# Two DeepNorm layers with 64 routed experts: fixed experts packed in three blocks, the slot table made on chip, the first norm tile by tile

## The chip, the core and the metric

The kernel runs on one core of one Trainium2 chip. The metric is the device time of one launch in microseconds (us). The matrix engine is PE (its weight loads PEld), the vector engine DVE, the activation engine ACT, GpSimd POOL, and SP issues most DMAs.

## What is computed

Two layers over 384 tokens (128 of a prompt, 256 of a sample) of width 1024, in float32. Each layer has a mixer (retention, windowed attention, neighbourhood attention) with one projection in and one out, a layer norm, and a mixture of experts with a second norm:

```python
scores = jax.nn.sigmoid(x @ w_router)                       # 384 x 64
emask  = ...                                                # 4 best of 8 groups
_, eidx = lax.top_k(jnp.where(emask, sel, NEG_INF), TOP_K)  # 6 experts a token
wsel = wsel / jnp.sum(wsel, -1, keepdims=True) * ROUTE_SCALE
...
gu  = x[tok] @ w_gu[e]                                      # 1024 -> 512
out = (jax.nn.silu(gu[:, :256]) * gu[:, 256:]) @ w_down[e]  # 256 -> 1024
routed = jnp.zeros_like(x).at[buf_tok].add(out * buf_w)
x = layer_norm(ALPHA * x + g2 * (routed + shared), ln2_g, ln2_b)
```

All 64 experts get tokens (2304 assignments, 36 an expert on average), so the weights of every expert are read in each layer: 2 MB for gate and up, 1 MB for down.

## The kernel before

Everything is written out by hand: five engine programs, one function for each engine in `run_layer`, tied by semaphores; each engine goes through its instructions in program order, and so does SP with its DMAs. The part that the change touches begins at the end of the mixer.

**First norm and routing.** PE multiplies by the output projection, token tile by token tile (L1027, three tiles of 128 tokens, two column halves each). DVE takes each half out of PSUM (L1539), adds the residual (L1508), takes the statistics (L1510 to L1513); ACT takes the root (L1966) and normalizes (L1968). `norm(0, from_psum)` does the statistics of all three tiles first; after it a loop modulates tile 0, 1 and 2 (L1548, L1549) for the experts. PE runs eight filler products (`keep_busy`, L788), then turns each modulated tile (L803), ACT copies it to `xmT` (L1852), and PE makes the router's logits (L1034): those of tile 0 after tiles 0 and 1 are turned, those of tiles 1 and 2 at the end. ACT's sigmoid (L1974) then starts the routing on DVE.

**Plan of the blocks.** Tokens are gathered in blocks of 128 rows. `plan_blocks` fixes beforehand how experts share blocks: experts 0 to 3 have a block of their own each, and the other 60 are ranked by their count of tokens and fill 28 blocks, with one expert (128 rows), two (64 and 64) or three (64, 32 and 32). There are 32 blocks a layer. Within a block the experts' products stand side by side in PE's columns, so that a block costs PE the same with one, two or three experts.

**Slot table.** The slots (which token stands in which row of which block, with what weight) of blocks 0 to 3 are made by one-hots on DVE (L1602) and products on PE (L1071). For the other 28 blocks DVE works out a place for each of the 18 assignments of a partition (L1653 to L1663); POOL writes the entries to a table in HBM with 18 indirect DMAs (L2091), waits for them, reads the table back (L2096), and DVE copies it to `slot_idx`, `slot_tok`, `slot_w` (`take_slots`, L1673 to L1675, after block 2). POOL gathers the rows of each block from `scratch_x` (L2077).

**The loop over blocks.** For block b PE does gate and up (`gate_up`, L1113), adds the rows of block b-2 to their tokens (L1163, L1164), turns the gathered rows of block b+1 (L1100), does down for block b-1 (L1140) and turns the hidden rows of block b (L1125); in between stand pieces of the shared expert (`SHARED_AT`). DVE multiplies the hidden rows (`hidden`, L1729) between gate-up and the turning.

**Weights.** SP loads gate-up weights into a ring of four slots and down weights into six. The load of expert n into its slot (L688) waits until the block of expert n-4 is through gate-up, a down load (L692) until the block of expert n-6 is through down. Experts 0 to 3 are loaded before the ranking is known.

Of the kernel before, what the change touches and what calls it, by code (L numbers as in the profile page):

```python
# [36 lines left out]
PRE = 4  # L37


def plan_blocks():  # L40

    blocks = [[(n, P)] for n in range(PRE)]
    wide, half, third = iter(range(PRE, 12)), iter(range(12, 40)), iter(range(40, E))
    for _ in range(4):
        for kind in (3, 1, 3, 2, 3, 1, 2):
            if kind == 1:
                blocks.append([(next(wide), P)])  # L50
            elif kind == 2:
                blocks.append([(next(half), 64), (next(half), 64)])
            else:
                blocks.append([(next(half), 64), (next(third), 32), (next(third), 32)])
    assert all(next(left, None) is None for left in (wide, half, third))
    return blocks
# [4 lines left out]
LOADS = [r for b in BLOCKS for r, rows in b]  # L61
BLOCK_OF = [n for n, b in enumerate(BLOCKS) for r in b]
# [4 lines left out]
SHARED_AT = {7 + 2 * t + step: (t, step) for t in range(TILES) for step in range(2)}  # L67
SHARED_AT.update({16 + 2 * t + f: (t, 2 + f) for t in range(TILES) for f in range(2)})
SHARED_LOAD, SHARED_DOWN_LOAD, NORM_LOAD = 4, 13, 24
# [25 lines left out]
def constants():  # L95
# [48 lines left out]
    cap, row, col = np.zeros(P), np.zeros(P), np.zeros(P)  # L144
    for n, b in enumerate(BLOCKS):
        for i, (r, rows) in enumerate(b):
            cap[r], row[r], col[r] = rows, sum(other for _, other in b[:i]), n
    put("cap", cap[:, None])
    put("first_row", row[:, None])
    put("column", col[:, None])  # L150
# [46 lines left out]
def build(nc, a, o):  # L197
    soft = [(m, t, h) for t in range(TILES) for m in "BC" for h in (0, 3)]

    with ExitStack() as ctx:  # L200
# [66 lines left out]
        table = c(NB * 2).rearrange("p (b v) -> p b v", v=2)  # L267
# [20 lines left out]
        one_hot = [[c(P) for _ in range(TILES)] for _ in range(PRE)]  # L288
# [6 lines left out]
        wsum = c(8)  # L295
        key_row, rank_at, home, away, room = c(E), c(E), c(E), c(E), c(E)
        key_col = c(2)
        assert c.at <= route_at + 2 * DM + 3 * F

        c = Carve(A, route2_at)  # L300
# [32 lines left out]
        lnb = c(2 * DM).rearrange("p (r d) -> p r d", r=2)  # L333
        shared_gu = B[:, c.at - 4 * DM:c.at].rearrange("p (k n) -> p k n", k=KD)
# [18 lines left out]
        over_part = [ring[3][:, 1536 + CH * (u % 4):2048 + CH * (u % 4)] for u in range(UNITS)]  # L353
        over_idx = nc.alloc_sbuf_tensor_at("over_idx", [P, PASSES * E], I32, offset=begins["ring3"] + 4 * 1024)[:]
# [14 lines left out]
        first_in = c(TILES * PRE * 2).rearrange("p (t e v) -> p t e v", t=TILES, v=2)  # L369
        first_pos = c(TILES * PRE).rearrange("p (t e) -> p t e", t=TILES)  # L370

# [47 lines left out]
        def run_layer(l):  # L419
# [15 lines left out]
            def of_layer(d, name):  # L435
# [27 lines left out]
            table_empty, entries_ready, entries_sent, table_loaded = (  # L463
                sem("table_empty"), sem("entries_ready"), sem("entries_sent"), sem("table_loaded"))
# [12 lines left out]
            first_gathered = [sem(f"first_gathered{b}") for b in range(PRE)]  # L477
# [49 lines left out]
            def gather_of(b):  # L527


                if b < PRE:  # L530
                    return (xg + [gateb[:, 0, :], gateb[:, 1, :]])[b], first_gathered[b], 16
                return xg[b % 2], gathered[b % 2], 16 * ((b - PRE) // 2 + 1)

            def block_loads(b):
                return [n for n in range(E) if BLOCK_OF[n] == b]

# [20 lines left out]
            def _(sp):  # L557
# [157 lines left out]
                for b in range(NB):  # L715
                    if b == 0:
                        sp.wait_ge(entries_ready, 1)
# [11 lines left out]
                    if b == SHARED_LOAD:  # L729
                        sp.wait_ge(residual_ready, TILES)  # L730
# [38 lines left out]
            def _(pe):  # L769
# [374 lines left out]
                def add_rows(b, units):  # L1144


                    for u in units:
                        t, f = u // 2, u % 2
                        bank = psum[UNIT_BANK[u]]
                        if u == 0:  # L1150
                            pe.wait_ge(to_token_ready, b + 1)
                            pe.wait_ge(ys_ready, 2 * (b + 1))
                            if b:
                                pe.wait_ge(added, UNITS * b - 1)
# [1014 lines left out]
```

## Time and profile before

| what | value |
|---|---|
| median of 3 runs (lowest, highest) | 1875.14 us (1873.4, 1878.14) |
| the profiled execution | 1875.72 us, of it 1873.7 us span |
| PE, DVE, ACT busy in the span | 90%, 44%, 21% |
| chain that ended last | PE 35%, DMA 6%, DVE 4% |
| first gate-up of layer 0 and of layer 1 | at 377.7 and 1290.7 us |

The span holds layer 0 up to about 960 us and layer 1 after it. The expert blocks take from 378 to 921 us and from 1291 to 1833 us. The profile's chain lists for each step what released it; its views by windows give the busy time, the clock that PE was granted (PEclk, 1.00 is 2.4 GHz) and the DMA engines' share in a stretch.

### The profile page before, as it was taken

What the parts mean: (1) busy time and instruction counts of PE and PEld (TensorE: products, weight loads), DVE (VectorE), ACT (ScalarE), POOL (GpSimd) and SP (SyncE); (2) the same over time, 40 slices, a digit from 0 to 9 for tenths busy, and PEclk for the clock granted to TensorE, in tenths of its full rate; (3) what the DMA queues carried; (4) which work ended last, traced back from release to release, by engine and by line L of the source; (5) the groups of instructions that cost most, each with busy time, mean ns of one, the idle gap of its engine ahead of it and who ended that gap; (6) DMA issues with size and microseconds to landing.
All of it is one profiled execution on the core that took longest, in us unless ns stands there. A gap on an engine that the chain in (4) does not pass through costs nothing. (4 is left out here: it accounts for less than half of the span.)

```text
span 1873.7 us, 22699 instructions
## 1 busy us (share of the span) xinstructions
PE 1686.7 (90%) x8463; PEld 919.4 (49%) x8463; DVE 819.7 (44%) x1652; ACT 389.6 (21%) x754; POOL 147.5 (8%) x144
## 2 busy tenths in 40 slices
PE   3999999999799799988979999899979989989794
PEld 1885654654344344343448756555434434434342
DVE  2435423654244344342583444255534343444346
ACT  1323531121111111111232324321111111111111
POOL 0000000240000000000010000013200000000001
PEclk8999989799899899999989999997989999999897
DMA  9534527558989999999634443453699899999990
GB/s 354 176 135 147 197 94 267 226 200 357 405 344 400 409 398 417 406 408 422 273 118 129 146 183 107 163 236 120 238 424 405 352 397 391 422 400 398 426 380 34
DMA packets 103470, 538.96 MB, mean 288 GB/s; under 512 B 36830, under 2 KB 39662, under 8 KB 64060
## 3 DMA queue, kind: packets, MB, share of 16 engines
q1 hardware_dynamic: 91996, 515.24, 69.4%
q0 software_dynamic: 11296, 22.14, 3.2%
q8 instruction: 70, 1.15, 0.2%
q14 instruction: 44, 0.36, 0.1%
q10 hardware_dynamic: 64, 0.07, 0.0%
HBM read 545.95 MB, written 6.59 MB: 295 GB/s over the span
## 5 line engine op out<-in xcount | busy, mean ns | idle before, releaser
L1113 PE MATMUL bank<-ring,arena_a 128*32 128x512 f32 (+2 forms) x2432 | 477.1, 632 | 78.4 <-DMA ring<-in_w_expert_gu 77.4
L1113 PEld LDWEIGHTS bank<-ring,arena_a 128*32 128x32 f32 (+2 forms) x2432 | 166.1, 134 | 356.8 <-issue 356.0
L1715 DVE TENSOR_TENSOR arena_a<-arena_a,bank 128x512 f32<-128x512 f32 x336 | 230.5, 686 | 9.7
L1729 DVE SCALAR_TENSOR_TENSOR arena_a<-arena_a,slot_w,bank 128x256 f32<-128x256 f32 x64 | 30.8, 481 | 444.6 <-ACT arena_a L1999 341.1
L1140 PE MATMUL bank<-arena_b,arena_a 128*32 128x512 f32 (+2 forms) x800 | 204.1, 596 | 8.3 <-issue 3.3
L1163 PE MATMUL bank<-ys_hi,to_token 128*128 128x512 f32 x348 | 153.7, 442 | 0.0
L1745 DVE TENSOR_TENSOR ys_lo<-bank,ys_hi 128x512 fp32r<-128x512 f32 x120 | 77.3, 686 | 141.4 <-ACT ys_hi L2007 141.2
L1164 PE MATMUL bank<-ys_lo,to_token 128*128 128x512 f32 x348 | 136.7, 393 | 0.0
L1999 ACT ACTIVATE arena_a<-bank 128x256 f32<-128x256 f32 x64 | 24.6, 384 | 525.8 <-PE bank L1113 525.8
L2077 POOL DMA_INDIRECT arena_a<-scratch_x,slot_idx x60 | 61.0, 1016 | 915.3 <-PE bank L1100 860.0
L881 PE MATMUL bank<-win_hi,xmT_hi 128*128 128x512 f32 (+1 forms) x288 | 109.9, 382 | 14.6 <-DVE arena_a L1335 10.4
L1140 PE MATMUL bank<-arena_a 128*32 128x512 f32 (+2 forms) x416 | 116.4, 595 | 4.4 <-issue 2.2
L2007 ACT ACTIVATE ys_hi<-bank 128x512 fp32r<-128x512 f32 x120 | 65.1, 595 | 218.1 <-PE bank L1140 218.1
L883 PE MATMUL bank<-w_lo,xmT_hi 128*128 128x512 f32 (+1 forms) x288 | 109.6, 381 | 0.0
L882 PE MATMUL bank<-win_hi,xmT_lo 128*128 128x512 f32 (+1 forms) x288 | 109.2, 379 | 0.0
L1140 PEld LDWEIGHTS bank<-arena_b,arena_a 128*32 128x32 f32 (+2 forms) x800 | 64.3, 129 | 76.4 <-issue 74.1
L1027 PE MATMUL bank<-ring,xmT 128*128 128x512 f32 x192 | 86.3, 612 | 6.3 <-ACTq L1961 6.3
L1163 PEld LDWEIGHTS bank<-ys_hi,to_token 128*128 128x128 f32 x348 | 65.4, 188 | 46.2 <-issue 36.3
L1316 DVE TENSOR_TENSOR w_lo<-ring,win_hi 128x2048 fp32r<-128x2048 f32 (+1 forms) x24 | 51.5, 2148 | 80.5 <-ACT win_hi L1867 78.4
L1991 ACT ACTIVATE arena_a<-bank 128x512 f32<-128x512 f32 x64 | 38.3, 598 | 192.2 <-PE bank L1100 192.2
L1164 PEld LDWEIGHTS bank<-ys_lo,to_token 128*128 128x128 f32 x348 | 65.7, 189 | 14.9 <-issue 4.8
L881 PEld LDWEIGHTS bank<-win_hi,xmT_hi 128*128 128x128 f32 x288 | 55.4, 192 | 25.3 <-issue 14.8
(304 smaller groups left out, 2014.7 us busy)
## 6 DMA issues: line engine op xcount, KB each, us to landing
ring<-in_w_expert_gu SPq DMA_DIRECT2D x128, 2048.0 KB, 13.2
arena_b<-in_w_expert_down SPq DMA_DIRECT2D x88, 1024.0 KB, 17.8
ring<-in_w_mod SPq DMA_DIRECT2D x24, 2048.0 KB, 7.8
arena_a<-in_w_expert_down SPq DMA_DIRECT2D x40, 1024.0 KB, 18.1
ring<-in_w_in SPq DMA_DIRECT2D x10, 2048.0 KB, 13.2
ring<-in_w_out SPq DMA_DIRECT2D x4, 2048.0 KB, 8.0
arena_b<-mods SPq DMA_DIRECT2D x8, 512.0 KB, 9.5
arena_a<-mods SPq DMA_DIRECT2D x8, 512.0 KB, 10.0
```

The source lines that it names most:

```text
L881: pe.matmul(out, hi[:, k, :], win_hi[:, k, cols], start=(k == 0), stop=False)
L882: pe.matmul(out, lo[:, k, :], win_hi[:, k, cols], start=False, stop=False)
L883: ins = pe.matmul(out, hi[:, k, :], w_lo[s][:, k, cols], start=False, stop=(k == KD - 1))
L1027: ins = pe.matmul(bank[:, :], xmT[:, k, P * t:P * t + P], w[:, k, :], start=(k == 0), stop=(k == KD - 1))
L1113: ins = pe.matmul(psum[0][r:r + w, :], xT[:, k, r:r + w], ring_view(gu_slot(n))[:, k, :], start=(k == 0), stop=(k == KD - 1))
L1140: ins = pe.matmul(psum[5 + f][r:r + w, :], hT[b % 2][:, k, r:r + w], down[n % ND][:, k, CH * f:CH * f + CH], start=(k == 0), stop=(k == 1))
L1163: pe.matmul(bank[:, :], rows_of, ys_hi[:, cols], start=True, stop=False)
L1164: pe.matmul(bank[:, :], rows_of, ys_lo[:, cols], start=False, stop=True).then_inc(added_full, 1)
L1715: ins = dve.tensor_tensor(z, z, bank[:, :], ALU.add)
L1745: dve.tensor_tensor(lo_of[b][:, cols], psum[5 + f][:, :], hi_of[b][:, cols].bitcast(F32), ALU.subtract).then_inc(ys_ready, 1)
L2007: act.activation(hi_of[b][:, CH * f:CH * f + CH], psum[5 + f][:, :], ACT.Copy).then_inc(ys_high, 1)
L2077: pool.indirect_dma_start(rows_in, None, scratch_x, bass.IndirectOffsetOnAxis(ap=slot_idx[:, b:b + 1], axis=0), bounds_check=TOK - 1, oob_ ...
```

## The change

Four edits, made together. The blocks: experts 0 to 3 get 96 rows each and share three blocks (0 with 1, 1 with 2, 2 with 3), the 60 ranked ones fill 26 blocks, most of them of two or three experts; there are 29 blocks. Expert 1 and expert 2 are used in two blocks, so their ring slots, like that of expert 3, are held up to block 1, 2 and 2. The table: DVE makes for each of the 18 assignments the block (as a row of 29 ones and zeros, with token and weight) and the row (a one-hot of 128), and PE multiplies and sums them in block 1 (`make_table`); POOL's 18 writes and the read go into the branch for overfull experts, which is taken only when an expert has more tokens than rows. Block 2 now needs that table, and is turned after it. The norm: tile 2 is done in halves, tiles 0 and 1 are normalized and modulated while PE multiplies for tile 2, the logits of tiles 0 and 1 come before those of tile 2, and the eight filler products become two. Pieces of the shared expert move two or three blocks ahead.

```diff
+    blocks = [[(0, 96), (1, 32)], [(1, 64), (2, 64)], [(2, 32), (3, 96)]]
+    single, wide, half, third = iter(range(PRE, 5)), iter(range(5, 12)), iter(range(12, 39)), iter(range(39, E))
+    for kind in (2, 4, 3) * 6 + (2, 3, 4, 3, 2, 3, 2, 1):
...
+        elif kind == 4:
+            blocks.append([(next(wide), 96), (next(third), 32)])
...
+LOADS = list(dict.fromkeys(r for b in BLOCKS for r, rows in b))
+BLOCK_OF = [max(i for i, b in enumerate(BLOCKS) if r in [other for other, _ in b]) for r in LOADS]
...
-                keep_busy(("xT", 1, 0, 0), 8)
                 for t in range(2):
-                    pe.wait_ge(xm_ready, t + 1)
                     turn_x(1, t, xm2)
                 pe.wait_ge(wr_loaded, 16)
                 bank = begin(("logit",))
                 logits(bank, 0)
-                pe.wait_ge(xm_ready, TILES)
+                logits(bank, 1)
+                keep_busy(("xT", 1, 2, 0), 2)
                 turn_x(1, 2, xm2)
-                logits(bank, 1)
                 end(logits(bank, 2), ("logit",))
...
+                def make_table():
+                    for t in range(TILES):
+                        pe.wait_ge(rows_hot, t + 1)
+                        for k in range(TOPK):
+                            j = TOPK * t + k
+                            ins = pe.matmul(psum[1][:, 0:2 * NB], in_row[t][:, k, :], placed[:, j].rearrange("p b v -> p (b v)"),
+                                            start=(j == 0), stop=(j == TILES * TOPK - 1))
+                    ins.then_inc(table_full, 1)
...
+                    if b == 1:
+                        make_table()
+                        emptied(5, 6)
+                        down_rows(0)
+                        turn_hidden(1)
+                        turn_rows(2)
+                        continue
...
+                statistics(0, 0, from_psum)
+                statistics(0, 1, from_psum)
+                modulate(0)
+                scale_shift(0, 1)
+                last_half(0)
+                modulate(1)
+                last_half(1)
...
+                scale_shift(0, 2)
+                modulate(2)
...
-                dve.tensor_copy(place_i[:], place).then_inc(entries_ready, 1)
...
+                link(dve.tensor_scalar(block_at, place, 1.0 / P, None, ALU.mult))
+                link(dve.tensor_tensor(past, over_blocks(block_at, NB + 1), columns(NB + 1), ALU.is_ge))
+                link(dve.tensor_reduce(column_at, past[:, :, 1:NB + 1], AX.X, ALU.add))
...
+                link(dve.tensor_tensor(in_block, past[:, :, 0:NB], past[:, :, 1:NB + 1], ALU.subtract))
...
+                    dve.tensor_tensor(in_row[t], const("slot").unsqueeze(1).to_broadcast([P, TOPK, P]),
+                                      row_at[:, TOPK * t:TOPK * t + TOPK].unsqueeze(2).to_broadcast([P, TOPK, P]), ALU.is_equal).then_inc(rows_hot, 1)
...
-                    dve.wait_ge(table_loaded, 16)
...
+                    dve.wait_ge(table_full, 1)
...
-                for j in range(TILES * TOPK):
-                    pool.indirect_dma_start(slots, bass.IndirectOffsetOnAxis(ap=place_i[:, j:j + 1], axis=0),
...
-                pool.dma_start(table, by_row[:, 0:NB, :]).then_inc(table_loaded, 16)
```

PE's program around block 1, before: block 2's rows were turned and its gate-up stood right behind down of block 0 and the turning of block 1's hidden rows (`ring` is the gate-up weights, `arena_b` the down weights).

```order
L1140 MATMUL bank<-arena_b,arena_a 128x512 [waits hT_ready,down_ready0,bank_free6,bank_free5]
L1140 MATMUL bank<-arena_b,arena_a 128x512 x3
L1125 MATMUL bank<-cst,arena_a 128x128 [waits hT_ready,hid_ready]
L1125 MATMUL bank<-cst,arena_a 128x128
L1113 MATMUL bank<-ring,arena_a 128x512 [waits ring_ready2,hid_ready,xT_ready]
```

The same place now: after gate-up of block 1 the 18 products of the table (L1127), down of block 0, and only then the turning of block 2's rows (L1118), which waits for their gather.

```order
L1141 MATMUL bank<-ring,arena_a 64x512 [waits ring_ready1,ring_ready2,hid_ready,xT_ready]
L1141 MATMUL bank<-ring,arena_a 64x512 x15
L1127 MATMUL bank<-arena_a,arena_b 128x58 [waits rows_hot]
L1127 MATMUL bank<-arena_a,arena_b 128x58 x5
L1127 MATMUL bank<-arena_a,arena_b 128x58 [waits rows_hot]
L1127 MATMUL bank<-arena_a,arena_b 128x58 x5
L1127 MATMUL bank<-arena_a,rows 128x58 [waits rows_hot]
L1127 MATMUL bank<-arena_a,rows 128x58 x5
L1168 MATMUL bank<-arena_b,arena_a 32x512 [waits down_ready0,hT_ready,down_ready1,bank_free6,bank_free5]
L1168 MATMUL bank<-arena_b,arena_a 32x512 x15
L1153 MATMUL bank<-cst,arena_a 128x128 [waits hT_ready,hid_ready]
L1118 MATMUL bank<-cst,arena_a 128x128 [waits xT_ready,gathered0]
```

So gate-up of block 2 now stands behind a gather that itself stands behind the table.

DVE's program at the end of the first norm, now, from the last column half of tile 2 (L1595) on: half the width is left to add and to take statistics of, and one modulation (L1583, L1586) instead of the three that stood here before.

```order
L1595 TENSOR_TENSOR arena_a<-bank,arena_b 128x512 [waits bank_full5,xm_ready]
L1597 SCALAR_TENSOR_TENSOR arena_a<-x,arena_a 128x512 [waits dve_step]
L1598 BN_STATS cmisc<-arena_a 128x6 [waits dve_step]
L1607 BN_AGGR cmisc<-cmisc 128x2 [waits dve_step]
L1608 TENSOR_SCALAR cmisc<-cmisc 128x1 [waits dve_step]
L1553 RECIPROCAL cmisc<-cmisc 128x1 [waits lroot_ready]
L1554 TENSOR_SCALAR cmisc<-cmisc 128x1 [waits dve_step]
L1583 TENSOR_TENSOR arena_a<-arena_a 128x1024 [waits normal_ready]
L1586 TENSOR_TENSOR arena_a<-arena_a 128x128x4 [waits dve_step]
L1586 TENSOR_TENSOR arena_a<-arena_a 128x128x4
```

The modulations of tiles 0 and 1 have moved ahead of the last column half, where DVE waited for PE.

## Rows read from the trace of the kernel before

**Rows 1.** The page: span, and its costliest group with the waits before it.

```profile
span 1873.7 us, 22699 instructions
...
L1113 PE MATMUL bank<-ring,arena_a 128*32 128x512 f32 (+2 forms) x2432 | 477.1, 632 | 78.4 <-DMA ring<-in_w_expert_gu 77.4
```

**Rows 2.** Windows, expert stages: length, PE/PEld/DVE/ACT/POOL busy (count), PEclk, DMA share, GB/s.

```profile
440.00:460.00 20.00, 19.74 (x103) 9.36 (x105) 9.42 (x20) 3.64 (x7) 0.99 (x1) 1.00 1.00 423
382.00:440.00 58.00, 57.10 (x245) 29.64 (x244) 29.23 (x54) 10.85 (x23) 23.44 (x23) 1.00 0.66 240
560.00:914.00 354.00, 323.19 (x1734) 149.14 (x1726) 141.64 (x270) 50.54 (x100) 17.79 (x18) 0.96 0.99 408
382.00:914.00 532.00, 488.97 (x2511) 228.81 (x2509) 215.04 (x409) 78.57 (x157) 47.16 (x47) 0.96 0.94 385
1296.00:1826.00 530.00, 484.52 (x2495) 225.17 (x2493) 214.83 (x406) 78.43 (x155) 47.90 (x47) 0.96 0.94 384
```

**Rows 3.** Timeline of PE, layer 0, blocks 2 and 3: start, us, engine, line.

```profile
398.40 7.03 PE L1113 MATMUL bank<-ring,arena_a 128*128 128x512 f32 x16
...
407.12 1.03 PE L1100 MATMUL bank<-cst,arena_b 128*128 128x128 f32 x8
...
409.47 3.67 PE L1140 MATMUL bank<-arena_b,arena_a 128*128 128x512 f32 x8 [0.39 <-DVE arena_a L1713]
413.19 7.03 PE L1113 MATMUL bank<-ring,arena_a 128*128 128x512 f32 x16
```

**Rows 4.** Timeline of the first norm's end in layer 1: DVE, PE, ACT.

```profile
1240.01 0.69 DVE L1539 TENSOR_TENSOR arena_a<-bank,arena_b 128x512 f32<-128x512 f32 x1 [5.61 <-PE bank L1027]
1242.11 1.29 DVE L1510 BATCH_NORM_STATS2 cmisc<-arena_a 128x6 f32<-128x512 f32 x2
...
1244.42 1.22 DVE L1548 TENSOR_TENSOR arena_a<-arena_a 128x1024 f32<-128x1024 f32 x1
1244.54 1.24 ACT L1968 ACTIVATE arena_a<-arena_a,cmisc 128x1024 f32<-128x1024 f32 x1 [0.48 <-DVE cmisc L1519]
1245.67 1.92 DVE L1549 TENSOR_TENSOR arena_a<-arena_a 128x1024 f32<-128x1024 f32 x1
...
1255.10 1.92 PE L803 MATMUL bank<-cst,arena_a 128*128 128x128 f32 x8
1256.80 4.54 PE L1034 MATMUL bank<-arena_a,xmT 128*128 128x64 f32 x32
1261.38 0.33 ACT L1974 ACTIVATE arena_a<-bank 128x192 f32<-128x192 f32 x1 [2.35 <-PE bank L1034]
```

**Rows 5.** Windows of layer 1 from the logits through the routing.

```profile
1250.00:1262.00 12.00, 11.15 (x66) 10.77 (x67) 4.28 (x6) 4.00 (x6) 4.71 (x6) 0.72 0.36 143
1272.00:1282.00 10.00, 10.00 (x44) 8.63 (x43) 4.53 (x22) 0.00 (x0) 0.00 (x0) 0.50 0.00 0
```

**Rows 6.** Timeline of layer 0: POOL's first table write and first table gather, DVE's first hidden rows.

```profile
382.48 1.02 POOL L2091 DMA_INDIRECT slots<-arena_a,place_i  x1 [7.85 <-DVE place_i L1663]
...
385.31 0.48 DVE L1729 SCALAR_TENSOR_TENSOR arena_a<-arena_a,slot_w,bank 128x256 f32<-128x256 f32 x1 [2.83 <-ACT arena_a L1999]
...
416.48 1.05 POOL L2077 DMA_INDIRECT arena_a<-scratch_x,slot_idx  x1 [6.11 <-DVE slot_w L1675]
```

**Rows 7.** DMA issues of the page: count, KB each, median us to landing.

```profile
ring<-in_w_expert_gu SPq DMA_DIRECT2D x128, 2048.0 KB, 13.2
...
arena_a<-scratch_x,slot_idx POOLq DMA_INDIRECT x60, 10.6
...
arena_b<-scratch_x,slot_idx POOLq DMA_INDIRECT x4, 3.5
```

**Rows 8.** The chain that ended last, layer 1, around a wait for weights: start, us, what.

```profile
1717.77 7.11 PE bank L1113 x64
1728.17 25.29 DMA ring<-in_w_expert_gu
1753.60 8.74 PE bank L1113 x64
```

More of the change, by code:

```diff
@@ L37 @@
 PRE = 4
+PREB = 2
+FIXED_ROOM = 96
+FIRST_PARTS = [(0, 0), (1, 0), (1, 1), (2, 1)]
+OVER = 4096
 def plan_blocks():
[L45 to L55, printed above, removed]
+    blocks = [[(0, 96), (1, 32)], [(1, 64), (2, 64)], [(2, 32), (3, 96)]]
+    single, wide, half, third = iter(range(PRE, 5)), iter(range(5, 12)), iter(range(12, 39)), iter(range(39, E))
+    for kind in (2, 4, 3) * 6 + (2, 3, 4, 3, 2, 3, 2, 1):
+        if kind == 1:
+            blocks.append([(next(single), P)])
+        elif kind == 4:
+            blocks.append([(next(wide), 96), (next(third), 32)])
+        elif kind == 2:
+            blocks.append([(next(half), 64), (next(half), 64)])
+        else:
+            blocks.append([(next(half), 64), (next(third), 32), (next(third), 32)])
+    assert all(next(left, None) is None for left in (single, wide, half, third))
     return blocks
@@ L266, in build @@
         hT = [c(F).rearrange("p (k t) -> p k t", k=2) for _ in range(2)]
-        table = c(NB * 2).rearrange("p (b v) -> p b v", v=2)
+        block_at, column_at, row_at = (c(TILES * TOPK) for _ in range(3))
         place, most_f = c(TILES * TOPK), c(8)
@@ L1086, in _ @@
                 pe.wait_ge(ranks_ready, 1)
-                for i, name in enumerate(("cap", "first_row", "column")):
+                for i, name in enumerate(("cap", "home")):
                     pe.matmul(bank[:, E * i:E * i + E], const(name)[0:E, :].to_broadcast([E, P]), rank_is[0:E, :], start=True, stop=True)
-                end(pe.matmul(bank[:, 3 * E:4 * E], const("up")[0:E, :].to_broadcast([E, P]), rank_at[0:E, :], start=True, stop=True), ("where",))
+                end(pe.matmul(bank[:, 2 * E:3 * E], const("up")[0:E, :].to_broadcast([E, P]), rank_at[0:E, :], start=True, stop=True), ("where",))
                 assert next(turn, None) is None
@@ L1542, in from_psum, with modulate @@
                             scale_shift(which, t - 1)
-                norm(0, from_psum)
-                for t in range(TILES):
+                def modulate(t):
                     c_ = 0 if t == 0 else 1
@@ L1845, in late_rows, with turned @@
                     act.dma_start(mods[:, n // 2, CH * (n % 2):CH * (n % 2) + CH], stage[n % 2]).then_inc(stage_sent[n % 2], 16)
[L1847 to L1848 removed]
+                def turned(*tiles):
+                    for t in tiles:
                         for g in range(2):
@@ L1961, in _, with norm @@
                     act.sem_inc(yT_ready, 1)
-                def norm(which):
-                    for t in range(TILES):
+                def norm(which, *tiles):
+                    for t in tiles:
                         act.wait_ge(lvar_ready, TILES * which + t + 1)
```

212 lines of the change are left out of this document (136 added, 76 removed).

## The prediction

> **What bounds the kernel now.** I read the page first, then windows, then the timeline at the three places that the change touches. The page shows PE as the busy engine and gate-up as its costliest line, with 78 us of idle time before it that ended with a weight load [rows 1]. So PE isn't the only limit. The windows say where the other one is [rows 2]: over layer 0's expert stage (382 to 914 us, from the first load of a ranked expert to the landing of the last) the DMA engines are 0.94 busy at 385 GB/s, and from 560 on 0.99 busy at 408 GB/s. Layer 1's stage looks the same (530 us, 0.94, 384 GB/s). The reader is to see that late in the stage nothing more fits into the queues, while the opening (382 to 440) has a share of 0.66 and 240 GB/s: there PE was nearly always busy (57.1 of 58 us) and the queues waited for ring slots.
>
> In this opening a block takes 14.8 us: gate-up starts at 398.40 and again at 413.19, with 7.03 us of gate-up, 3.67 of down and 1.03 for turning rows, the rest being additions [rows 3]. Three blocks fewer are therefore 3 x 14.8 = 44.4 us of PE a layer. How much of that is time depends on the weights, whose bytes don't change.
>
> As bytes: 532 us x 385 GB/s = 204.8 MB; at 408 GB/s these need 502 us, so 30 us of layer 0's stage are lost to an idle queue. The opening moved 58 x 240 = 13.9 MB, worth 34 us, so 24 of the 30 are lost there; the other 6 come later.
>
> Measurement tells a change of 0.3% (5.6 us) from none. My sums are made against the profiled execution (1875.72 us, 1873.7 of it the span [rows 1]); the median of the runs is 0.6 us below it.
>
> **The norm.** Before, DVE gets PE's last column half at 1240.01 and the sigmoid starts at 1261.38: 21.4 us [rows 4], in which PE waits. After the change what is left behind that half is: gating 0.69, residual on half the width 0.69 (the gating has that size), one of two statistics 0.65, the small steps up to ACT 1.1 (1243.40 to 1244.54), normalizing 1.24, multiplying 1.22, the addition in two halves 1.92, the second half's turning 0.96 (half of 1.92), ACT's copy 0.6 (half a normalization), one tile's logits 2.27 (half of 4.54), and six hand-overs between engines, for which I allow 0.15 each (0.04 lie between the last logits and the sigmoid), 0.9 [rows 4]. That is 12.2 us, a gain of 9.2. Tiles 0 and 1 are modulated where DVE sat idle for 5.61 us [rows 4] and earlier. Against it: ACT copies four half tiles (2.5 us) ahead of the last root, and PE's two fillers stand ahead of tile 2. Low end 6 us, high end 10.5 (PE at the full clock); I take **9**, near the sum. The sums of the keys, ranks and counts that follow change by less than 1 us beside PE's work and are costed at nothing; if PE ran faster there, DVE's longer list of first slots (four small instructions for one) would show, 0.6 us.
>
> The eight fillers that go are the other side. PE was granted 0.72 of its clock over 1250 to 1262 and 0.50 over 1272 to 1282 even with them [rows 5], so the lengths above are already those of a PE that is partly at 1.2 GHz, and taking the fillers away can cost the matrix part (0.96 + 2.27) once more at most; the low end holds that.
>
> **The table.** POOL's 18 writes, the wait and the read (from 382.48 until the first gather from the table at 416.48 [rows 6]) go. They weren't on PE's path, since block 4 was the first to need them, but block 2 now is. DVE's new list: five instructions of 522 or 540 elements at 0.7 (512 take 0.69), three of 768 at 0.95 (between 0.69 for 512 and 1.22 for 1024) [rows 4] and a few small ones, 6.9 us, less some 2 for ten small ones that go: 4 to 7, I take 5. DVE was idle for 2.83 us before the first hidden rows at 385.31 [rows 6], so these come at 387.5, 2.2 late, and so does gate-up of block 1 (388.7 to 395.8, in the clock of layer 0 before). The table is 18 products of two passes each; 36 x 0.142 (4.54 / 32 [rows 4]) = 5.1 us, up to double at the lower clock: 400.9. Down of block 0 and turning take 4.1: PE is free at 405. The gather is issued at 401.5 and lands 3.5 us (few other loads) to 10.6 us (the queues full) later [rows 7], at 405 to 412; I take 408, since only one weight load is under way. Turning 1.03 [rows 3], ACT's copy 1.2 and hand-overs: gate-up of block 2 runs from 410.5 to 417.6. Before, block 2 ran at 398.40 and block 3 until 420.2 [rows 3]: with a block fewer the change is 2.6 us ahead there.
>
> **The weight stream.** Up to the end of block 2 only two ring slots come free (after blocks 0 and 1), because the slots of experts 2 and 3 are held. From 382 to 419.6 (417.6 and an estimated 2 us until packets flow, below the 3.5 us in which the quickest gathers land [rows 7]) the queues get two gate-up and two down loads, 6.3 MB (2048 KB a gate-up load [rows 7], half of that a down load), and some 0.6 MB of gathers: 17 us of work at 408 GB/s, so 20.6 are lost, less 2 because the places are ready that much earlier. After that the stream should not stop: three blocks take seven experts, 22 MB and 1 MB of gathers, 56 us, against 3 x 14.8 = 44.4 of PE; I allow 2 us. Lost: 18.6 + 2 = 21 instead of 30, **9 a layer**, and 1 off for a tail in which the last block stands further behind its weights: **8**. So 44.4 us of PE work buy 8, and the rest becomes waiting for weights at gate-up: that is late next. The shared expert's pieces, 2 or 3 blocks earlier, cost nothing under these waits; without them they'd be the same work at another place.
>
> Low end of this part: 0, with a gather of 10.6 us, a table at twice its price; high end 26: all 204.8 MB at the 423 GB/s of 440 to 460 [rows 2], 484 us.
>
> By the Trainium skill (DMA: Bandwidth & Descriptors, Specifications) a core gets about 358 GB/s of HBM; the stage would need 204.8 / 0.358 = 572 us whatever the blocks, and only the norm's gain would be left. The trace doesn't agree: 408 GB/s were held for 354 us [rows 2], and the sum goes by that.
>
> **Sum.** 2 x (9 + 8) = 34; 1875.7 - 34 = 1841.7, and 1841 for the median.
>
> **Rivals.**
> - *The stream runs full.* If a queue that never empties runs at 423 GB/s throughout [rows 2], 18 us a layer more: 1841 - 36 = 1805. For it: every idle gap lowers the 408 too. Against: at a share of 0.99 there is little to gain. Chance 0.20.
> - *The weights swallow the blocks.* A late gather of block 2 and a table at the lower clock (0.50 in the stretch before it [rows 5]) lose in the opening what the three blocks give; only the norm's 9 a layer stay: 1875 - 18 = 1857. For it: PE waits for weights already [rows 1], and block 2's chain has no cover. Against: it takes both at their high ends. Chance 0.20.
> - *Slower: waits lower the clock, and the ring feels it.* With 56 us of weights to 44.4 of PE some 20 blocks a layer wait. After a wait of 25.29 us gate-up took 8.74 us, not 7.11 [rows 8], and its slots come free 1.6 us later. If the queue is empty by then, each such wait lengthens the stage: 20 x 1.63 = 33 us a layer, 1841 + 66 = 1907; from 13 such waits a layer (2 x (17 - 13 x 1.63) + 0.3%) it is slower than before. For it: the rows. Against: two or three down loads (2.6 us each) stand in the queue behind the gate-up loads and keep it fed over 1.6 us, and the 408 already holds such waits. Chance 0.05. By the Trainium skill (TensorE: Matmul & The Clock Gate, HAM oscillation) a matmul loop that waits for loads falls back to the lower clock each time; the trace agrees (8.74 against 7.11 [rows 8]).
> - *The change doesn't do what it says.* More tokens than rows would start the branch for overfull experts, 192 passes long. The reference's own routing gives at most 68 tokens to a fixed expert (96 rows), 107 to the first ranked one (128), 55 to rank 12 (64 rows), 29 to rank 39 (32 rows). Chance 0.01.
>
> **Chances and range.** The forecast, 1826 to 1856, has 0.51; the two faster rivals 0.20 each; both gains lost to small things, within 0.3%, 0.03; slower 0.05 + 0.01. Faster is 0.51 + 0.20 + 0.20 = 0.91, same 0.03, slower 0.06. The range reaches to 1808 (most of the first rival lies above or near it) and to 1864 (the second rival and a norm at its low end, 1875 - 12 = 1863); about 2 in 10 stay outside.
>
> **What would show it.** Right: sigmoid to last column half some 12 us, not 21; 29 groups of gate-up a layer; DMA share near 1 from block 3 to the end, 0.4 to 0.5 before; idle time before gate-up that ends with weights well over 78 us; gate-up of block 2 some 33 us behind that of block 0. Wrong: a stage shorter than 500 us (first rival), of 530 or more (second), or DMA gaps right after long waits at gate-up (third); or POOL's table writes in the trace.

## The result, and the profile after

The changed kernel takes 1830.25 us (median of 4 runs, 1826.82 to 1832.7) where the kernel before takes 1876.64 (1873.4 to 1882.23): a ratio of 0.9748, 95% interval 0.9718 to 0.9779, faster. The prediction was 1841 with 1826 to 1856 for the forecast. A second set of runs, on another occasion, gave 1831.85 and 0.9757 (0.9732 to 0.9783).

The profiled execution has 46.9 us less span than before [rows 1]. The page of the changed kernel, its span, chain and costliest group:

```profile
span 1826.8 us, 23899 instructions
...
PE 32%; DMA 9%; DVE 5%; ACT 1%; issue 1%; SPq 0%; ACTq 0%; DVEq 0%; POOLq 0%
...
L1141 PE MATMUL bank<-ring,arena_a 128*32 128x512 f32 (+2 forms) x2976 | 446.7, 644 | 114.1 <-DMA ring<-in_w_expert_gu 111.3
```

Gate-up is busy for 446.7 us, not 477.1 [rows 1], and waits 111.3 us for weights, not 77.4: in both layers together gate-up is 30 us shorter, and 34 us of new waiting for weights came. Where the 46.9 us went, by marks in the two timelines:

| stretch | before, us | after, us | gained |
|---|---|---|---|
| start to the first output product, layer 0 | 285.7 | 280.9 | 4.8 |
| PE's end of the last column half to sigmoid, layer 0 and 1 | 21.4, 21.4 | 12.1, 12.0 | 18.7 |
| sigmoid to first gate-up, layer 0 and 1 | 27.4, 29.3 | 27.6, 27.5 | 1.6 |
| first to last gate-up, layer 0 and 1 | 543.5, 542.4 | 532.4, 532.3 | 21.2 |
| all else | 402.5 | 402.0 | 0.5 |

The expert stage, windows of the changed kernel (length, busy time of PE, PEld, DVE, ACT and POOL with counts, PEclk, DMA share, GB/s); they answer to [rows 2]:

```profile
367.00:425.00 58.00, 54.16 (x364) 24.94 (x360) 29.22 (x53) 8.83 (x20) 4.95 (x5) 0.97 0.71 274
425.00:540.00 115.00, 108.95 (x658) 47.54 (x651) 43.98 (x85) 16.67 (x34) 5.95 (x6) 0.99 0.99 407
540.00:888.00 348.00, 295.77 (x1863) 127.66 (x1865) 126.21 (x240) 45.33 (x89) 15.86 (x16) 0.93 0.99 408
367.00:888.00 521.00, 458.89 (x2880) 200.14 (x2876) 199.41 (x378) 70.82 (x141) 26.76 (x27) 0.94 0.96 393
1258.00:1779.00 521.00, 458.25 (x2864) 198.34 (x2856) 199.53 (x379) 70.57 (x139) 27.23 (x27) 0.95 0.95 391
```

521 us at 393 GB/s are the same 204.8 MB. The queue is full from 425 on at the same 408 GB/s as before; only the opening has a hole (0.71), and PE is now 85% busy late in the stage, where it was 91%. In the kernel before, the queue lost some us after its opening too, in this stretch:

```profile
440.00:560.00 120.00, 108.67 (x539) 50.03 (x541) 44.17 (x87) 17.18 (x34) 5.93 (x6) 0.96 0.93 386
```

The opening of layer 0, timeline of PE, DVE and POOL:

```profile
363.60 7.07 PE L1141 MATMUL bank<-ring,arena_a 128*32 128x512 f32 x64 [0.30 <-issue]
...
374.38 7.09 PE L1141 MATMUL bank<-ring,arena_a 128*64 128x512 f32 x32
381.40 2.89 PE L1127 MATMUL bank<-arena_a,arena_b 128*128 128x58 f32 x24
384.12 1.50 PE L1127 MATMUL bank<-arena_a,rows 128*128 128x58 f32 x12
385.56 3.64 PE L1168 MATMUL bank<-arena_b,arena_a 128*32 128x512 f32 x32
...
390.76 1.10 PE L1118 MATMUL bank<-cst,arena_a 128*128 128x128 f32 x8 [1.19 <-DMA arena_a<-scratch_x,slot_idx]
393.03 8.77 PE L1141 MATMUL bank<-ring,arena_a 128*32 128x512 f32 x64 [1.17 <-ACT arena_a L2098]
...
373.42 0.47 DVE L1832 SCALAR_TENSOR_TENSOR arena_a<-arena_a,slot_w,bank 128x256 f32<-128x256 f32 x1
...
386.80 0.99 POOL L2185 DMA_INDIRECT arena_a<-scratch_x,slot_idx  x1 [28.22 <-DVE slot_w L1753]
```

The chain is the one foretold: table, gather, turning, gate-up of block 2. PE waits twice in it, 1.19 and 1.17 us, and gate-up then takes 8.77 us instead of 7.09 (over 393.6 to 403.6 us PE was granted 0.85 of its clock).

The end of the first norm in layer 1, timeline of DVE, PE and ACT, from the last column half to the sigmoid; it answers to [rows 4]:

```profile
1214.71 0.69 DVE L1595 TENSOR_TENSOR arena_a<-bank,arena_b 128x512 f32<-128x512 f32 x1 [0.99 <-PE bank L1046]
1215.55 0.69 DVE L1597 SCALAR_TENSOR_TENSOR arena_a<-x,arena_a 128x512 f32<-128x512 f32 x1
...
1219.89 1.23 DVE L1583 TENSOR_TENSOR arena_a<-arena_a 128x1024 f32<-128x1024 f32 x1 [1.31 <-ACT arena_a L2072]
1221.15 1.95 DVE L1586 TENSOR_TENSOR arena_a<-arena_a 128x512 f32<-128x512 f32 x2
...
1224.60 2.00 PE L1053 MATMUL bank<-arena_a,xmT 128*128 128x64 f32 x16 [0.73 <-ACTq L1959]
...
1226.63 0.33 ACT L2080 ACTIVATE arena_a<-bank 128x192 f32<-128x192 f32 x1 [0.75 <-PE bank L1053]
```

11.9 us from 1214.71 to 1226.63 (12.0 from PE's end, as in the table). The chain of waits late in layer 1 (1600 us to the end; first its shares by line, then one piece of it: start, us, what):

```profile
by line: DMA ring<-in_w_expert_gu 49.6%; PE bank L1141 42.7%; PE bank L1168 2.0%; SPq L728 1.9%; issue 1.6%; PE bank L1193 0.9%; PE bank L1194 0.8%; PE bank L1118 0.5%; SPq L704 0.3%; PE bank L1153 0.2%
...
1675.79 8.05 DMA ring<-in_w_expert_gu
1683.84 0.14 issue
1683.97 7.11 PE bank L1141 x64
1691.10 0.27 SPq L728
1691.39 0.15 SPq L728
1691.82 13.29 DMA ring<-in_w_expert_gu
1705.24 9.77 PE bank L1141 x64
```

This is a loop: gate-up lets a ring slot go, SP issues the load into it, gate-up of a later block waits for that load. Both halves of the loop are in the chain, although the queue is full all the while. So a longer gate-up here is not free, and a faster PE elsewhere is not worth its whole time. A load's length in this chain runs from its issue to its landing; PE's own wait, in its timeline, is shorter:

```profile
1683.97 7.07 PE L1141 MATMUL bank<-ring,arena_a 128*32 128x512 f32 x64 [0.91 <-DMA ring<-in_w_expert_gu]
...
1705.24 9.73 PE L1141 MATMUL bank<-ring,arena_a 128*32 128x512 f32 x64 [6.27 <-DMA ring<-in_w_expert_gu]
```

The granted clock was 1.00 in the first of these gate-ups and 0.72 in the second.

### The profile page after: what moved, and what is told of

It is laid out like the page before. It is cut to its first block and busy times, and to the rows that moved or that the text cites. A ratio compares the mean times of both kernels' runs of the same rounds, so it can differ in the third digit from the quotient of the medians.

```text
span 1826.8 us, 23899 instructions
## 1 busy us (share of the span) xinstructions
PE 1607.3 (88%) x9191; PEld 848.1 (46%) x9191; DVE 790.5 (43%) x1598; ACT 374.5 (20%) x724; POOL 98.6 (5%) x96
## 5 line engine op out<-in xcount | busy, mean ns | idle before, releaser
L1141 PE MATMUL bank<-ring,arena_a 128*32 128x512 f32 (+2 forms) x2976 | 446.7, 644 | 114.1 <-DMA ring<-in_w_expert_gu 111.3
L1141 PEld LDWEIGHTS bank<-ring,arena_a 128*32 128x32 f32 (+2 forms) x2976 | 138.0, 124 | 394.8 <-issue 392.0
L1818 DVE TENSOR_TENSOR arena_a<-arena_a,bank 128x512 f32<-128x512 f32 x300 | 205.7, 686 | 8.7
L1168 PE MATMUL bank<-arena_b,arena_a 128*32 128x512 f32 (+2 forms) x1040 | 189.3, 595 | 5.1 <-DVE arena_a L1841 2.1
L1193 PE MATMUL bank<-ys_hi,to_token 128*128 128x512 f32 x312 | 132.8, 426 | 0.0
L1848 DVE TENSOR_TENSOR ys_lo<-bank,ys_hi 128x512 fp32r<-128x512 f32 x108 | 69.5, 686 | 125.5 <-ACT ys_hi L2113 125.4
L1194 PE MATMUL bank<-ys_lo,to_token 128*128 128x512 f32 x312 | 123.1, 394 | 0.0
L1168 PE MATMUL bank<-arena_a 128*32 128x512 f32 (+1 forms) x448 | 101.7, 595 | 1.5 <-issue 0.2
L1168 PEld LDWEIGHTS bank<-arena_b,arena_a 128*32 128x32 f32 (+2 forms) x1040 | 56.4, 116 | 84.2 <-issue 81.6
L1118 PE MATMUL bank<-cst,arena_a 128*128 128x128 f32 x464 | 62.0, 278 | 3.1 <-DMA arena_a<-scratch_x,slot_idx 3.1
## 6 DMA issues: line engine op xcount, KB each, us to landing
arena_b<-in_w_expert_down SPq DMA_DIRECT2D x88, 1024.0 KB, 18.5
arena_a<-mods SPq DMA_DIRECT2D x8, 512.0 KB, 10.3
```

What stands on the lines that cost most here:

```text
L1118: ins = pe.transpose(psum[2 + k // 4][:, P * (k % 4):P * (k % 4) + P], rows_in[:, P * k:P * k + P], ident)
L1141: ins = pe.matmul(psum[0][r:r + w, :], xT[:, k, r:r + w], ring_view(gu_slot(n))[:, k, :], start=(k == 0), stop=(k == KD - 1))
L1168: ins = pe.matmul(psum[5 + f][r:r + w, :], hT[b % 2][:, k, r:r + w], down[n % ND][:, k, CH * f:CH * f + CH], start=(k == 0), stop=(k == 1))
L1193: pe.matmul(bank[:, :], rows_of, ys_hi[:, cols], start=True, stop=False)
L1194: pe.matmul(bank[:, :], rows_of, ys_lo[:, cols], start=False, stop=True).then_inc(added_full, 1)
L1818: ins = dve.tensor_tensor(z, z, bank[:, :], ALU.add)
```

## The experiments

Times are medians; "of before" is the ratio to the kernel before on the same chip, with its 95% interval.

**The changed kernel once more, for comparison.** 

> The changed kernel as it is, for comparison on the same chip: 1830 us, 1826 to 1833. If the 4.8 us that the changed kernel's mixer of layer 0 was quicker belong to the change, the first output product of layer 0 starts 5 us sooner than in the kernel before here too; if they are chance of the clock, it can stand anywhere within those 5 us.

1831.85 us, 0.9757 (0.9732 to 0.9783). In its profiled execution the first output product of layer 0 stood at 286.7 us, where the first profile had 280.9 and the kernel before 285.7. The other eleven profiles of this study, whose mixers are the same, fall into the same two groups, whatever the kernel: 280.5 to 281.7 in seven of them, 285.6 to 286.3 in four. So the 4.8 us in the table above aren't the change's. Windows of the two first profiles (before, then after) show what differs, PE's clock (0.76 and 0.88):

```profile
250.00:285.00 35.00, 30.21 (x175) 17.35 (x173) 3.57 (x12) 13.65 (x32) 0.00 (x0) 0.76 0.16 61
```

```profile
250.00:281.00 31.00, 24.52 (x171) 14.13 (x163) 3.16 (x9) 13.45 (x32) 0.00 (x0) 0.88 0.18 69
```

The expert stage differs between the two profiles of the changed kernel as well. The second was taken of an execution of 1842.21 us, and its stages are 538.3 and 532.5 us long, where the first has 532.4 and 532.3: gate-up of block 1 alone took 8.49 us in layer 0 and not 7.09, at a granted clock of 0.83. So what the stage of layer 0 gained is between 5 and 11 us, that of layer 1 is 10 us in both, and a difference of a few us between single profiles in the runs that follow isn't shown to be of the edit.

**The norm undone in the changed kernel.** DVE's and ACT's order, the whole-tile modulation, the logits and eight fillers as before:

```diff
+                keep_busy(("xT", 1, 0, 0), 8)
...
-                logits(bank, 1)
-                keep_busy(("xT", 1, 2, 0), 2)
                 turn_x(1, 2, xm2)
+                logits(bank, 1)
...
-                statistics(0, 0, from_psum)
-                statistics(0, 1, from_psum)
...
+                norm(0, from_psum)
+                for t in range(TILES):
+                    modulate(t)
```

> The changed kernel with the first norm, its modulation, the eight fillers and the order of the logits as in the kernel before; blocks and table stay as changed. Theory (PE waits for the norm, and nothing behind it makes up for a later start): last column half to sigmoid 21.4 us again, 9.4 a layer more, 1849 (1845 to 1852). Rival (the expert stage, bound by weights whose first loads wait already, gives part of it back): under 1840.

1859.22 us, 0.9902 (0.9873 to 0.9931): 0.0145 x 1876 = 27 us more than the changed kernel, not 19. From the last column half to the sigmoid it is 21.6 us in both layers, 19 us more together, as expected, and the expert stage gives nothing back (534.8 and 534.1 us against 532.4 and 532.3). In the profiled execution (1869.19 us, 10 above this run's median) another 12 us lie between the experts of layer 0 and the output products of layer 1, in code that wasn't touched, where PE was granted 0.78 and 0.74 in two stretches and the changed kernel 0.97 and 0.91.

**The norm alone in the kernel before.** The same edit the other way. 

> The kernel before with the new norm alone (order of the norm, half tiles, logits, two fillers); 32 blocks and the table through memory. Theory (the norm is worth its own stretch, 9.4 us a layer, in either kernel): 1857 to 1858. Rival (the 27 us that its undoing cost in the changed kernel are all its own): 1849.

1851.5 us, 0.9882 (0.9860 to 0.9904): 22 us less than the kernel before. Its norm takes 12.3 and 12.0 us, 18.5 of the 24.3 us by which its profiled span is shorter; 4.0 are the mixer of layer 0 again (281.7), and 3.2 the stretch from sigmoid to gate-up. Its expert stages are those of the kernel before (543.8 and 543.3 us). So the norm's gain takes nothing from the experts' and is 18.5 to 19 us by its own stretch in both kernels; whether the 3 to 8 us beyond it belong to the norm (a PE that waits less, and keeps its clock) or to chance isn't settled by these two runs.

**The old plan with the new table and norm.** 

> The changed kernel with the plan of the kernel before: 32 blocks, one fixed expert each, the shared expert's pieces at their old blocks; norm and table stay as changed. Theory (the weights set the pace; three blocks fewer are worth what the opening's queue loses without them): with one ring slot a block, 402 to 432 us of layer 0 moves some 5 MB instead of 12, so 17 us a layer are lost there: 1864 (1852 to 1876). Rival (PE sets the pace, and the blocks' 44.4 us a layer are time): 1918.

```diff
-FIXED_ROOM = 96
-FIRST_PARTS = [(0, 0), (1, 0), (1, 1), (2, 1)]
+FIXED_ROOM = 128
+FIRST_PARTS = [(0, 0), (1, 1)]
...
-    blocks = [[(0, 96), (1, 32)], [(1, 64), (2, 64)], [(2, 32), (3, 96)]]
+    blocks = [[(n, P)] for n in range(PRE)]
```

1869.97 us, 0.9954 (0.9936 to 0.9972): 38 us above the changed kernel, so three blocks fewer, with the shared expert's pieces moved along with them (this run puts those back too), are worth 19 us a layer, not 44. The run also prices the table, since its plan is that of before. PE in the opening:

```profile
361.36 7.11 PE L1140 MATMUL bank<-ring,arena_a 128*128 128x512 f32 x16 [0.36 <-issue]
...
389.96 1.09 PE L1117 MATMUL bank<-cst,arena_a 128*128 128x128 f32 x8 [0.89 <-DMA arena_a<-scratch_x,slot_idx]
392.23 7.13 PE L1140 MATMUL bank<-ring,arena_a 128*128 128x512 f32 x16 [1.18 <-ACT arena_a L2097]
```

Gate-up of block 2 starts 30.9 us behind that of block 0, where the kernel before has 20.7 (398.40 [rows 3] less 377.7). The stage is 554.6 and 552.3 us long, 10 to 11 more than before, and that difference is there by block 7 (115.1 against 104.9 us) and stays to the end. With 32 blocks, then, the table on the chip is a loss of 10 us a layer in this profile. The times say somewhat less: this run is the kernel before with the new norm and the new table, the last one the kernel before with the new norm alone, and 0.9954 less 0.9882 is 13.5 us, 7 a layer. The fewer blocks pay for it and bring 10 to 12 us on top.

**The table twice.** `for t in list(range(TILES)) * 2` in `make_table`. 

> The 18 products of the table are made twice, the second time into the same bank from the start. That is 4.2 us more of PE between gate-up of block 1 and the gather for block 2. Theory (block 2 has no cover, and the next two weight loads wait for its end): gate-up of block 2 ends 4.2 us later, the two loads behind it start 4.2 us later, and the end of the stage moves by the same: 8.4 us in all, 1838 to 1839. Rival (the waits for weights later in the stage swallow what the opening loses): no change, 1830.

1838.77 us, 0.9805 (0.9776 to 0.9834), some 7 to 9 us above the changed kernel, as the theory said, but the intervals touch and the profile doesn't show it where it should be: gate-up of block 2 ended 1.2 us later in layer 0 and 3.4 in layer 1, not 4.2, since it started 2.9 and 4.9 us later and took 7.1 us in both, not 8.8 and 8.6 (why it was quicker isn't shown); the two stages (530.3 and 535.0 us) are together 0.6 us longer than those in the first profile of the changed kernel; 10 us lie between the layers (285.6 us for 275.6), where nothing was edited. What the table's products cost, between nothing and their 4.2 us a layer, isn't settled.

**Fillers in each block.** 

> The changed kernel with eight filler products (128x512) ahead of each gate-up from block 3 on, after its wait for rows and before its wait for weights: 26 x 8 x 0.214 = 44.5 us of PE a layer more, about what three blocks cost. Theory (from block 3 on the weights set the pace, and PE's idle time before gate-up, 55 us a layer, takes the fillers): at most 6 us a layer more, 1830 to 1842. Rival (PE sets the pace): 89 us more, 1919.

```diff
+                    if b > 2:
+                        for _ in range(8):
+                            pe.matmul(psum[0][:, :], ident, cst[:, 0:CH], start=True, stop=True)
                     for n in loads:
                         pe.wait_ge(ring_ready[gu_slot(n)], 16 * gu_loads(n))
```

2046.26 us, 1.0898 (1.0865 to 1.0931), 214 more than the changed kernel. The expectation had the price of a filler wrong, as the page of this run shows (832 records, two to a product, 365.6 us: 0.88 us a product, not 0.214):

```profile
L1144 PE MATMUL bank<-ring,arena_a 128*32 128x512 f32 (+2 forms) x2976 | 418.2, 603 | 2.4 <-ACT arena_a L2101 2.3
L1139 PE MATMUL bank<-cst 128*128 128x512 f32 x832 | 365.6, 592 | 0.0
```

So 366 us of work were put in and 214 came out. Most of the other 152 are what the changed kernel had left on PE: the 111 us of waits for weights (all gone, 2.4 of any kind are left) and 28 us of gate-up at a lower clock (446.7 to 418.2). Here PE is the limit, and the stream isn't:

```profile
425.00:888.00 463.00, 461.25 (x2413) 199.55 (x2415) 141.88 (x272) 51.91 (x102) 19.77 (x20) 1.00 0.83 336
```

**Two fillers instead of eight.** 

> As the run with eight fillers, but with two: a product of 128x512 in this kernel is 7.07 / 8 = 0.88 us (gate-up is eight of them), not the 0.214 that the first expectation took, so 26 x 2 x 0.88 = 46 us of PE a layer, what three blocks cost. Theory (PE's idle time before gate-up, 55 us a layer, takes them): at most 7 us a layer more, 1830 to 1845. Rival (PE sets the pace): 92 us more, 1922.

1856.83 us, 0.9912 (0.9891 to 0.9934): 25 more by the medians and 29 by the ratios, 12 to 15 a layer, for 49 us of fillers a layer (97.8 us in the page's group). A quarter to 30% comes through, more than the 7 us that were allowed: half of the waits for weights (52.5 us) are still there, but the fillers stand in the loop of ring slots also where weights had landed. Neither engine alone sets the pace at this point.

**Half the bytes.** The load of each expert beyond those in the first ring and down slots is cut to its first half, in the changed kernel and in the one before. 

> The changed kernel with half the bytes: from the fifth expert on only half of a gate-up load and from the seventh on half of a down load is made, so the products use old weights in the other half (that part of the computation is left out). Theory (with weights out of the way PE sets the pace): idle time before gate-up that ends with weights falls from 111 us to under 15, and the time to 1715 to 1740.

> The kernel before with the same half loads (the same part of the computation left out). Theory (the three blocks are real PE time that the weights hide): 80 to 108 us slower than the changed kernel with half loads, instead of the 46 that it is with full loads: 1800 to 1840. Rival (the blocks save no more PE time than was seen): 46 us slower than that kernel.

1691.28 us (0.9017, 0.8943 to 0.9090) and 1780.41 us (0.9492, 0.9419 to 0.9564). The pages, first the changed kernel, then the one before:

```profile
L1143 PE MATMUL bank<-ring,arena_a 128*32 128x512 f32 (+2 forms) x2976 | 413.8, 598 | 4.6 <-ACT arena_a L2100 2.3
```

```profile
L1115 PE MATMUL bank<-ring,arena_a 128*32 128x512 f32 (+2 forms) x2432 | 452.2, 594 | 0.9 <-ACT arena_a L1994 0.6
```

With no waits for weights the two kernels are 89 us apart, not 46, and their stages 457.5 and 461.4 against 491.3 and 491.2 us: 32 us a layer, about three blocks of 14.8 less the table's chain. So the change takes that much off PE, and the waits for weights (71 to 75 us a layer above this floor in the changed kernel, 51 or 52 in the one before) hide two thirds of it. Both times are some 20 us below what was expected, their difference is not.

**Earlier loads in the opening.** The queue's hole in the changed kernel lies at 0.62 and 0.16 from 383.6 to 403.6 us, because SP stands at the wait for block 2. 

> Only SP's order is changed: the shared expert's gate-up weights (2 MB) and the first down load whose slot comes free (1 MB) are issued before SP waits for the end of gate-up of block 2, not behind the two loads that wait for it. Theory (what the opening leaves the queue idle is lost for the stage): 3 MB at 408 GB/s, 7.4 us a layer, move into the idle part at 389 to 402 us, and each layer's stage is 5 to 7.5 us shorter: 1815 to 1820. Rival (the stage's length is set later, by PE or by waits in the middle): 1830, no change. Rival (the early loads disturb the gather for block 2 or 3): slower than 1830.

1825.29 us, 0.9729 (0.9704 to 0.9754): about 5 us less, a third to a half of the expectation, and the intervals overlap, so the time alone doesn't show it. Windows of 10 us, before and after the point where the changed kernel's hole ended:

```profile
387.90:397.90 10.00, 8.40 (x73) 5.23 (x71) 3.58 (x11) 1.29 (x3) 1.98 (x2) 1.00 0.82 281
397.90:407.90 10.00, 9.07 (x67) 2.61 (x68) 3.98 (x4) 1.27 (x3) 1.98 (x1) 0.83 0.85 300
407.90:417.90 10.00, 9.84 (x49) 4.89 (x49) 6.83 (x13) 2.17 (x4) 0.99 (x1) 1.00 1.00 401
417.90:427.90 10.00, 9.94 (x58) 4.95 (x58) 4.76 (x9) 1.47 (x3) 0.99 (x1) 1.00 0.63 229
```

The early 3 MB did move, and then the queue was dry again for 3.7 us, since block 3 had not yet let its slots go. Block 6 started 3.9 us sooner than in the changed kernel (100.3 against 104.2 after block 0; 4.1 sooner in layer 1), which is what 7.4 us won and 3.7 given back would leave.

**Three moves in the opening.** The table ahead of gate-up of block 1, the residuals and loads earlier still:

```diff
+                    if b == 1:
+                        make_table()
                     gate_up(b)
...
                         residual(0)
+                        take_slots()
                         residual(1)
...
+                    if b in (1, 2):
+                        sp.wait_ge(y_full, BLOCK_OF[b - 1] + 1)
+                        load_down(ND + b - 1, loaded(ND + b - 1))
```

> Three moves in the opening of the changed kernel: PE makes the table ahead of gate-up of block 1 (in the 1.3 us in which it waits, and 3 more) and turns block 2's rows ahead of down of block 0; DVE adds the last two residuals before the hidden rows of block 1, so that SP can issue the shared expert's 2 MB at about 384 us, ahead of the second ranked gate-up load; two down loads are issued as soon as their slots are free. Theory (the run with early loads gained 3.9 us a layer by block 6 and not 7.4, because its queue ran dry again at 421 to 424, before gate-up of block 3 let the next loads go): with the loads 10 us earlier and gate-up of block 2 ending 3 to 4 us sooner the queue should not run dry after 384: 7 to 10 us a layer off the changed kernel, 1810 to 1817. Rival (each hole only moves to the next place): 1823 to 1827, as with early loads alone.

1820.94 us, 0.9720 (0.9698 to 0.9742): 9 to 11 us below the changed kernel by the medians, 5 to 7 by the ratios, and the best of all versions, though its interval still overlaps that of the changed kernel. Block 6 starts at 97.4 us, 6.8 sooner (94.5 in layer 1, 10.3 sooner). The profiled execution took 1814.05 us, the least of the five. The ranked experts' weights take 515.5 and 507.7 us from the first issue to the last landing, against 519.3 and 519.5 (525.5 and 519.3 in the second profile of the changed kernel).

**Two more down loads earlier.** 

> The run with three moves in the opening left one hole: from 429.5 to 434 us of layer 0 the queue moved 12 and 81 GB/s, because SP waits for gate-up of block 4 while two more down slots have been free since 424. Here these two down loads (2 MB, 4.9 us at 408 GB/s) go ahead of that wait. Theory (a hole in the opening is lost for the stage): 4 to 5 us a layer off that run, 1811 to 1814 by its median of 1820.9. Rival (from here on PE or the waits in the middle set the pace): no change, 1821.

1829.46 us, 0.9752 (0.9724 to 0.9780): by the medians the gain is lost again, though this interval and that of the run with three moves overlap. Windows of the run with three moves, then of this one:

```profile
429.00:434.00 5.00, 5.00 (x40) 2.90 (x30) 2.29 (x4) 0.38 (x1) 0.00 (x0) 1.00 0.37 102
...
452.00:456.00 4.00, 4.00 (x30) 1.61 (x23) 1.62 (x5) 1.09 (x2) 0.00 (x0) 1.00 1.02 434
```

```profile
429.00:434.00 5.00, 5.00 (x52) 1.43 (x44) 0.30 (x1) 0.00 (x0) 0.00 (x0) 1.00 1.00 418
...
440.00:452.00 12.00, 9.43 (x64) 3.25 (x64) 1.86 (x5) 1.08 (x2) 0.00 (x0) 0.86 0.97 408
452.00:456.00 4.00, 4.00 (x28) 2.31 (x21) 1.79 (x4) 0.38 (x1) 0.00 (x0) 1.00 0.34 68
```

The hole at 429 is filled and stands at 452 now. The down loads that used to queue behind the gate-up loads were gone by then; block 5 had waited for its weights, its gate-up took 8.8 us and not 7.1, and nothing was left in the queue to cover it. Block 6 starts at 102.5 us. In layer 1 it is the same: block 5 waited 3.7 us, took 9.8, and the queue moved nothing from 1343 to 1346 us. But not all of the loss is the edit's: gate-up of block 2, ahead of the edited loads, already started at 31.5 and 30.0 us after block 0, where the run with three moves had 30.0 and 26.7. That leaves 3.6 and 5.4 of the 5.1 and 8.7 us by which block 6 was later.

## Why the prediction was right

The sum said 34 us and the profiled span lost 46.9; the median, 1830.25, lies inside the forecast of 1826 to 1856, 4 us above its low end and 11 below the 1841 of the sum. The mechanism was right and the gain was put too low. Of the 13 us between the two sums 4.8 are the mixer's clock in one profile, 5.2 the stream's term, and the rest small. The medians lie as far apart (46.4 us), which one profile's mixer doesn't explain: by the times the norm alone is worth 22 us in the kernel before, not 18, and table and blocks together 25 (0.9882 less 0.9748), not 16.

- *The norm*, "12.2 us, a gain of 9.2": 12.0 and 11.9 us counted as there, from DVE's start, a gain of 9.4. The working by rows held, small steps included, and a later start of the experts gives nothing back.
- *The table*: hidden rows of block 0 at 9.8 us after the block's start, as predicted (387.5 less 377.7), gate-up of block 1 at 10.8 (11.0). "36 x 0.142 = 5.1 us" was 4.23 (381.40 to 385.63), and the gather landed 3.9 us after its issue (386.80, landed 390.7), not the 6.5 taken: block 2 started 29.4 us behind block 0, not 33. What the prediction missed is the clock: its gate-up took 8.77 us, so it ended at 38.2, 1.7 us before the time predicted (39.9). In the run with 32 blocks it took 7.13 us behind the same two waits, so the slow one isn't certain.
- *The net of table and block*, "2.6 us ahead": both parts are larger than this net shows, a loss of 7 to 10 us a layer and a gain of 19 to 22, by the run with 32 blocks. The prediction didn't price them apart; that two parts without a price of their own left a net of about the right size is partly luck.
- *The stream*, "lost: 18.6 + 2 = 21 instead of 30": in the opening 58 us x 274 GB/s = 15.9 MB were worth 39 us at 408, so 19 were lost there, and none later (502 + 19 = 521). Gain by the weights 11.4 and 9.7 us (530.7 to 519.3, 529.2 to 519.5), by the blocks 11.1 and 10.2. The term of 8 was mis-sized by 2 or 3: the 6 us lost after the opening in the kernel before (most of them from 440 to 560 us, at 386 GB/s) went as well, not only 4 of them, and no tail was lost. In the second profile layer 0's stage gained 5.2 us, so for that layer the 8 lie between the two profiles.
- *"So 44.4 us of PE work buy 8, and the rest becomes waiting for weights"*: right in kind. The half loads put PE's saving at 32 us a layer, the table's chain taken off, of which 10 to 11 were bought.
- *The first rival* (423 GB/s throughout) didn't come: 408 over 348 us, as before, though stretches of 4 to 12 us in the runs reach 425 to 434.
- *The second* (the weights swallow the blocks) had the right places and too high a price for them: the table does eat 7 to 10 of the some 20 us a layer that the blocks bring, but its products and its gather were quicker than taken, and the opening lost no more than 19.
- *The third* (slow gate-ups after waits, and an empty queue) has its mechanism in the trace, but with 8 gate-ups of 8.5 to 10 us a layer after waits for weights, not 20 (14 a layer waited), and the queue stayed full behind them. The prediction argued that down loads in the queue would see to that; the last experiment took two of them out from behind the gate-up loads and got just such a hole at block 5. One reading behind this rival was wrong: the 25.29 us in [rows 8] are the load from issue to landing, while PE itself waited 6.02 us, as its timeline in the kernel before shows; gate-up was slower behind a wait of that size.

```profile
1753.60 8.70 PE L1113 MATMUL bank<-ring,arena_a 128*32 128x512 f32 x64 [6.02 <-DMA ring<-in_w_expert_gu]
```

The stage held 408 GB/s over 348 us. By the Trainium skill (HBM Reference, Specifications) the 358 GB/s a core, by which the prediction priced the stage once, are the share of a core whose neighbour streams too, and a core alone reaches some 425; the trace agrees in that its 408 GB/s lie above the share, and what the neighbour did no run here shows.

In the chain shown above gate-up took 9.73 us at a granted clock of 0.72 behind a wait of 6.27 us, and 7.07 at 1.00 behind one of 0.91. By the Trainium skill (TensorE: Matmul & The Clock Gate, HAM oscillation) a loop that waits for loads falls back to the lower clock each time; the trace agrees in part: of the 14 gate-ups a layer that waited for weights, 8 were slower.

## What to carry to other kernels

Where a stream of weights is full over most of a stage, price a saving on the engine by what it takes off the stream's idle time, and measure that idle time where it lies; here 32 us of PE a layer were worth 10 to 11 in the first profile. Price a new dependency and a saving that nets with it apart, since one of them can be had without the other. A hole in a queue that is fed by slots can move in place of closing: of the three runs with earlier loads two kept some of the gain up to block 6, and the third lost most of what the second had. So before issuing loads earlier, ask what they covered where they stood.

## What was not expected of the hardware

PE's clock differs between executions of the same code: the first output product of layer 0 stood at 280.5 to 281.7 us in eight profiles and at 285.6 to 286.7 in six, and the untouched stretch from the experts of layer 0 to the output products of layer 1 took 275.5 to 287.7 us, with granted clocks of 0.74 to 0.97 in parts of it. The expert stage of layer 0 took 532.4 and 538.3 us in two executions of the changed kernel. A single profile of this kernel is therefore good to some 5 to 10 us in its sum and to some 6 us in a stage, while a short stretch such as the end of the new norm took 11.9 to 12.5 us in all eleven profiles that have it.
